# Strassen-like row stage of a float32 block: where the operand sums are made, the order of the products, and who sums the weights

## The chip, the cores and the metric

The kernel runs on one core of a Trainium2 chip. Its time is the device time of the whole program in microseconds (us), the median of several executions.

## The reference, cut to what matters

Three transformer-like blocks run one after the other on x of 1024 positions by 1024 channels, all in float32. The change lies in the first block's feed-forward layer and in the step from there to the second block:

```python
D_FF = 2816
hn = rmsnorm(h, norm_ffn[l])
g, up = jnp.split(hn @ w_ffn_in[l], 2, axis=-1)
h = h + (jax.nn.silu(g) * up) @ w_ffn_out[l]
...
return rmsnorm(h, norm_final)
```

The second block begins with a projection `u = x @ w_in`, whose first column block holds the gates of an mLSTM.

## The kernel before

Activations lie transposed in SBUF: a tile has 128 channels on the partitions and 1024 positions along them. `h` has eight such tiles. Every float32 product is made as three float32r matmuls of 128x128 by 128x512: high part of the weights by high part of the operand, high by low, low by high. ScalarE makes the high part of the weights (`w_hi`, an ACTIVATE copy), GpSimd the low part (`w_lo`, a subtraction), and VectorE the low part of the operand.

**Column pairs (L1587).** The hidden layer is 22 tiles. Two are made in the plain way, the rest in 20 column pairs (a gate and an up block) by seven products on quarter matrices, as Strassen and Winograd do it. `mixed_pair` takes 84 matmuls a pair, twelve a product. Product j waits for `half_split`, GpSimd's low half of its weights; products 2 and 4 also wait until ScalarE has copied a bank away (`snapped`). Four half tiles of weights form a ring. `mixed_pair_scalar` is the order written out for ScalarE: w_hi of products 2 and 3, wait until the hidden tile of the pair before is made (`hid_made`), snapshot 1, then `behind_snap`, then w_hi 4 and 5, snapshot 3, w_hi 6, snapshot 5, w_hi 0 of the next pair, the silu, w_hi 1. The store of the hidden tile to `hid_dram` stands in `behind_snap`. GpSimd's `split_pair` makes three weight sums and seven low halves for each pair. VectorE (`pair_vector`) joins banks and makes the hidden tile, `act_g` for even tiles and `act_h` for odd ones.

**Row stage (L1650).** The second product of the layer, hidden by `w_ffn_out`, is again seven products on quarters: even and odd hidden tiles, low and high positions, even and odd output tiles. Each product i has 11 parts, 77 steps in all, and a step is twelve matmuls (four feature pairs m of three). Weights come in pieces (512 KB for two) through a ring of four blocks. Products 1 to 4 need sums of operand quarters; VectorE makes them in the stage (`sum_part`, L2181 to L2190), from hidden quarters loaded as wholes. Products 1, 2, 4 and 6 need sums of weights, also by VectorE (`sum_weights`, L2204 to L2213). Part and weight tiles are in rings of four: step s is rounded when step s - 3 has begun. When a product is full, `add_product` adds its four banks to h.

**Norm and gates.** ScalarE makes x_hi and the square of each tile of h, VectorE x_lo and the sum of squares; odd tiles come first. TensorE waits until all additions are made (`rows_added`), releases the weights (L531), and makes the gates block and the next block as a pair of interleaved blocks (`feature_pair`, L545), with the mean of the squares (`raw_mean`, L1551) behind tile 6. GpSimd splits both blocks behind the row stage. Behind the mean, ScalarE makes `first_root`, and VectorE scales three tiles of h, then makes `gate_rows` (L2605), on which the next block's bank and the gates' chain (soft, `log_f`, scans) wait.

## Time and profile before

| | |
|---|---|
| median of 3 executions | 3338.17 us (3336.87 to 3340.07) |
| profiled execution | 3340.51 us, span 3338.4 us |
| TensorE busy | 3194.8 us, 96% |
| VectorE, ScalarE, GpSimd busy | 1973.4, 1152.1, 1632.6 us |

The span runs from the first to the last instruction of the profile; times in its views count from its start. PE is TensorE, DVE VectorE, ACT ScalarE, POOL GpSimd, SP the engine that issues most loads; ACTq is the issue of a DMA on ScalarE. An engine's busy share over the whole span says little of a stage, so the rows below are of stages. The column pairs lie at 770 to 1154 us, the row stage at 1157 to 1373, the gates behind it.

### The profile page before, as it was taken

What the parts mean: (1) busy time and instruction counts of PE and PEld (TensorE: products, weight loads), DVE (VectorE), ACT (ScalarE), POOL (GpSimd) and SP (SyncE); (2) the same over time, 40 slices, a digit from 0 to 9 for tenths busy, and PEclk for the clock granted to TensorE, in tenths of its full rate; (3) what the DMA queues carried; (4) which work ended last, traced back from release to release, by engine and by line L of the source; (5) the groups of instructions that cost most, each with busy time, mean ns of one, the idle gap of its engine ahead of it and who ended that gap; (6) DMA issues with size and microseconds to landing.
All of it is one profiled execution on the core that took longest, in us unless ns stands there. A gap on an engine that the chain in (4) does not pass through costs nothing.

```text
span 3338.4 us, 41113 instructions
## 1 busy us (share of the span) xinstructions
PE 3194.8 (96%) x15258; PEld 2532.7 (76%) x15258; DVE 1973.4 (59%) x2372; ACT 1152.1 (35%) x1893; POOL 1632.6 (49%) x975
## 2 busy tenths in 40 slices
PE   8999999989999999889999899999999989999997
PEld 6776678768888778778876678888888858767775
DVE  6325645785333488797866673333333468988735
ACT  5435511043333334433323352222222341333351
POOL 5771134438888755413322147676676743333332
PEclk9999999999999999999999999999999999999998
DMA  3232014112222463131111121111111211111111
GB/s 120 104 116 69 34 49 182 49 33 76 85 84 82 154 212 101 46 95 58 64 37 35 37 82 60 41 60 52 50 58 43 89 51 39 43 43 50 42 32 70
DMA packets 72042, 236.11 MB, mean 71 GB/s; under 512 B 7792, under 2 KB 8432, under 8 KB 70896
## 3 DMA queue, kind: packets, MB, share of 16 engines
q1 hardware_dynamic: 54800, 162.03, 15.2%
q10 hardware_dynamic: 17120, 72.40, 5.8%
q8 instruction: 83, 1.36, 0.2%
q14 instruction: 39, 0.32, 0.0%
HBM read 203.46 MB, written 30.94 MB: 70 GB/s over the span
## 4 chain that ended last, share of the span: by engine, by line
PE 74%; DVE 13%; issue 4%; ACT 4%; POOL 3%; DMA 2%; ACTq 0%; DVEq 0%; POOLq 0%; SPq 0%
PE acc L1587 26%; PE acc L503 24%; PE acc L1603 7%; PE acc L523 5%; PE acc L1650 3%; PE acc L971 2%; PE acc L945 2%; POOL w_lo L3569 1%; DVE conv_slots L3127 1%; PE acc L595 1%; PE acc L545 1%; PE acc L922 1%; POOL raw L3564 1%; ACT band_probs L1086 1%; DVE h L1137 1%
## 5 line engine op out<-in xcount | busy, mean ns | idle before, releaser
L3554 POOL TENSOR_TENSOR w_hi<-raw,zero 128x1024 fp32r<-128x1024 f32 x107 | 219.0, 2047 | 1155.5 <-PE acc L503 551.5
L3569 POOL TENSOR_TENSOR w_lo<-raw,w_hi 128x512 fp32r<-128x512 f32 x318 | 488.5, 1551 | 206.3 <-ACT w_hi L1685 206.0
L1137 DVE TENSOR_TENSOR h<-h,acc 128x1024 f32<-128x1024 f32 x240 | 292.5, 1221 | 163.6 <-PE acc L1603 120.7
L3558 POOL TENSOR_TENSOR w_lo<-raw,w_hi 128x1024 fp32r<-128x1024 f32 x114 | 320.7, 2813 | 105.0 <-ACT w_hi L2522 96.6
L1685 ACT ACTIVATE w_hi<-raw 128x512 fp32r<-128x512 f32 x318 | 191.0, 625 | 410.4 <-POOL raw L3564 148.9
L1587 PE MATMUL acc<-x_hi,w_hi 128*128 128x512 f32 x812 | 316.3, 390 | 4.0 <-POOL w_lo L3569 1.4
L1587 PE MATMUL acc<-x_hi,w_lo 128*128 128x512 f32 x812 | 316.0, 389 | 0.0
L1587 PE MATMUL acc<-x_lo,w_hi 128*128 128x512 f32 x812 | 316.0, 389 | 0.0
L3564 POOL TENSOR_TENSOR raw<-raw 128x512 f32<-128x512 f32 x159 | 241.6, 1520 | 68.8 <-DMA raw<-blocks 58.5
L503 PE MATMUL acc<-x_hi,w_hi 128*128 128x512 f32 x816 | 257.0, 396 | 16.4 <-POOL w_lo L3558 4.5
L1587 PE MATMUL acc<-t_hi,w_hi 128*128 128x512 f32 x672 | 262.3, 390 | 3.4 <-POOL w_lo L3569 2.3
L1587 PE MATMUL acc<-t_lo,w_hi 128*128 128x512 f32 x672 | 261.6, 389 | 0.0
L1587 PE MATMUL acc<-t_hi,w_lo 128*128 128x512 f32 x672 | 261.5, 389 | 0.0
L503 PE MATMUL acc<-x_lo,w_hi 128*128 128x512 f32 x816 | 253.3, 392 | 0.0
L503 PE MATMUL acc<-x_hi,w_lo 128*128 128x512 f32 x816 | 252.8, 391 | 0.0
L3127 DVE SCALAR_TENSOR_TENSOR conv_slots<-conv_slots,par 128x1024 f32<-128x1024 f32 x120 | 227.5, 1896 | 4.1
L503 PEld LDWEIGHTS acc<-x_hi,w_hi 128*128 128x128 f32 x816 | 152.5, 189 | 51.9 <-issue 15.2
L2023 DVE TENSOR_TENSOR act_g<-high_sum,acc 128x512 f32<-128x512 f32 x33 | 22.7, 688 | 274.5 <-ACT high_sum L1693 274.4
L1587 PEld LDWEIGHTS acc<-x_hi,w_hi 128*128 128x128 f32 x812 | 152.4, 188 | 37.2 <-issue 4.1
L503 PEld LDWEIGHTS acc<-x_lo,w_hi 128*128 128x128 f32 x816 | 154.3, 189 | 32.7
L503 PEld LDWEIGHTS acc<-x_hi,w_lo 128*128 128x128 f32 x816 | 154.3, 189 | 32.6
L1587 PEld LDWEIGHTS acc<-x_hi,w_lo 128*128 128x128 f32 x812 | 152.4, 188 | 31.8
(498 smaller groups left out, 6824.7 us busy)
## 6 DMA issues: line engine op xcount, KB each, us to landing
raw<-blocks SPq DMA_DIRECT2D x189, 512.0 KB, 3.6
raw<-blocks SPq DMA_DIRECT2D x106, 256.0 KB, 2.6
raw<-row_pieces SPq DMA_DIRECT2D x22, 512.0 KB, 3.5
piece_block<-row_pieces SPq DMA_DIRECT2D x22, 512.0 KB, 3.5
hid_dram<-act_g ACTq DMA_DIRECT2D x11, 512.0 KB, 2.6
hid_dram<-act_h ACTq DMA_DIRECT2D x10, 512.0 KB, 2.6
h<-x_t ACTq DMA_DIRECT2D x8, 512.0 KB, 8.8
h<-x_t ACTq DMA_DIRECT2D x2, 2048.0 KB, 13.2
```

The costliest lines, as they stand in the source:

```text
L503: ins = pe.matmul(acc[s][:, c], w[:, slot, tile, :], part[:, c], start=(n == 0 and m == 0), stop=(n == last and m == 2))
L523: ins = pe.matmul(acc[s][:, c], w[:, slot, k, :], part[:, k, c], start=(k == 0 and m == 0), stop=(k == KT - 1 and m == 2))
L1137: dve.tensor_tensor(h[:, j, :], h[:, j, :], acc[s], ALU.add).then_inc(acc_free[s], 1)
L1587: ins = pe.matmul(bank, half_tile(w, at_, k), part[:, k, :], start=(begins and k == 0 and m == 0), stop=(k == QUARTER - 1 and m == 2), ski ...
L1603: ins = pe.matmul(acc[s][:, c], half_tile(w, (first + half) % 4, 2 * j + n), part[:, c], start=(n == 0 and m == 0), stop=(n == 1 and m == 2))
L1650: ins = pe.matmul(row_bank(i, m), row_half(w, step, m), x, start=(ROWS_BEGIN[i] and part == 0 and n == 0), stop=(part == ROW_PARTS - 1 and ...
L1685: act.activation(half_tile_range(w_hi, (2 * p + j) % 4), source.rearrange("p (a b) -> p a b", b=P), ACT.Copy)\
L3127: ins = dve.scalar_tensor_tensor(out=out, in0=shifted, scalar=weight, in1=out, op0=ALU.mult, op1=ALU.add)
L3554: pool.tensor_tensor(hi, raw[:, slot, :], nothing, ALU.add).then_inc(hi_split, 1)
L3558: pool.tensor_tensor(lo, raw[:, slot, :], hi.bitcast(F32), ALU.subtract).then_inc(w_split, 1)
L3564: pool.tensor_tensor(out, in0, in1, op).then_inc(sums_made, 1)
L3569: pool.tensor_tensor(half_tile_range(w_lo, at_), halves(source), half_tile_range(w_hi, at_).bitcast(F32), ALU.subtract).then_inc(half_spli ...
```

## The change

The operand sums are made among the column pairs: after every second pair VectorE makes three sums and a difference from the quarters of the two hidden tiles (`sum_hidden`, four operations of 128x512), and ScalarE stores the tiles and the three sums to `hid_dram` (seven slots of 256 KB a part) in three DMAs, behind a wait for `hid_summed`. The last of the eleven is stored by SP. In the row stage each step's operand comes from there through a ring of eight (`load_part`), and no step sums operands.

The order of the steps is a list: products 0 to 4, parts 0 to 2 of product 5, all of product 6, then the rest of product 5, whose weights and operand need no sum. The weight difference of product 6 is made by GpSimd (`sum_pieces`). The last three steps are interleaved by feature pair. Two blocks for the gates are loaded and split during the stage, at steps 36 to 56, into tiles of their own (`first_hi`, `first_lo`). TensorE waits for the additions of six products only and has no release matmul; the mean stands behind tile 4. ScalarE rounds the two blocks that follow before it makes the root, and VectorE scales one tile of h instead of three ahead of `gate_rows`.

```diff
+PART_RING = 8
+ROWS_TOGETHER = 3
+PART_SLOT = (0, 4, 5, 6, 1, 2, 3)
+FIRST_LOADED, FIRST_ROUNDED = (36, 50), (42, 56)
...
+ROW_ORDER = [(i, part) for i, first, after in ((0, 0, ROW_PARTS), (1, 0, ROW_PARTS), (2, 0, ROW_PARTS), (3, 0, ROW_PARTS),
+                                               (4, 0, ROW_PARTS), (5, 0, 3), (6, 0, ROW_PARTS), (5, 3, ROW_PARTS))
+             for part in range(first, after)]
+ROW_DONE = (0, 1, 2, 3, 4, 6, 5)
+
+
+def last_step(i):
+    return ROW_ORDER.index((i, ROW_PARTS - 1))
...
+        hidden_sums = at("hidden_sums", 132, [P, 3, HALF])
+        part_ring = [at(f"early_part{i}", 144 + 2 * i, [P, HALF])[:, :] for i in range(PART_RING)]
+        part_ring += [at(f"part{i}", 24 + 8 * (i // 2) + 2 * (i % 2), [P, HALF])[:, :] for i in range(PART_RING)]
+        late_squares = at("late_squares", 124, [P, KT // 2, TOK])
+        first_stage = at("first_stage", 184, [P, TOK])
+        first_hi = at("first_hi", 160, [P, 2, KT, P], F32R)
+        first_lo = at("first_lo", 168, [P, 2, KT, P], F32R)
...
-            for step in range(ROW_STEPS):
-                i, part = divmod(step, ROW_PARTS)
+            for step in range(ROW_STEPS - ROWS_TOGETHER):
                 if step == ROW_PARTS:
                     pe.wait_ge(snapped, t.count("snap"))
                     pe.wait_ge(joined, t.count("join"))
-                pe.wait_ge(row_split, step + 1)
-                pe.wait_ge(part_made, step + 1)
-                hi, lo = row_part_hi[step % ROW_RING], row_part_lo[step % ROW_RING]
-                for m in range(FEATURE_PAIRS):
+                row_steps(pe, [step])
+            row_steps(pe, range(ROW_STEPS - ROWS_TOGETHER, ROW_STEPS))
+            pe.wait_ge(rows_added, FEATURE_PAIRS * (PRODUCTS - 1))
+
+        def row_steps(pe, steps):
+            for m in range(FEATURE_PAIRS):
+                for step in steps:
+                    i, part = ROW_ORDER[step]
+                    if m == 0:
+                        pe.wait_ge(row_split, step + 1)
+                        pe.wait_ge(part_made, step + 1)
                     if i >= 2 and part == 0:
                         pe.wait_ge(rows_added, FEATURE_PAIRS * (i - 2) + m + 1)
+                    hi, lo = row_part_hi[step % ROW_RING], row_part_lo[step % ROW_RING]
...
+            pe.wait_ge(rows_added, FEATURE_PAIRS * (PRODUCTS - 1))
...
-            def store(n, b):
-                act.dma_start(hid_dram[:, bass.ds(n, 1), :].rearrange("p a n -> p (a n)"), hidden_of[b][:, :])\
-                   .then_inc(hid_out[b], 16)
-
-            def store_first(b):
-                act.wait_ge(hid_made, t.count("hid_made"))
-                store(b, b)
+            def store(part):
+                act.wait_ge(hid_summed, t.next("hid_summed"))
+                for out, (source, first, after) in zip(hid_out, hidden_parts):
+                    act.dma_start(hid_dram[:, bass.ds(part, 1), first:after, :].rearrange("p a b n -> p (a b) n"), source)\
+                       .then_inc(out, 16)
 
             def pair(b, follow, stored, behind_snap=None):
                 def store_last():
-                    if stored is not None:
-                        store(stored, 1 - b)
                     if behind_snap is not None:
                         behind_snap()
+                    if stored is not None:
+                        store(stored)
...
 
-            pair(0, "pair", 1, round_last)
-            pair(1, "pair", 2)
+            pair(0, "pair", 0, round_last)
+            pair(1, "pair", None)
...
-                act.wait_ge(dve_summed, ROW_PARTS * (1, 2, 4, 6).index(i) + part + 1)
+            if i in (1, 2, 4):
+                act.wait_ge(dve_summed, ROW_PARTS * (1, 2, 4).index(i) + part + 1)
+            elif i == 6:
+                act.wait_ge(pool_summed, part + 1)
             else:
                 await_piece(act, row_piece(step))
...
+            act.wait_ge(part_in[step % PART_RING], 16 * (step // PART_RING + 1))
+            act.activation(row_part_hi[step % ROW_RING], part_at(step), ACT.Copy).then_inc(part_high, 1)
+
+        def part_at(step):
+            return part_ring[step if step < PART_RING else PART_RING + step % PART_RING]
+
+        hidden_parts = ((act_g[:, :].rearrange("p (a n) -> p a n", a=2), 0, 2),
+                        (act_h[:, :].rearrange("p (a n) -> p a n", a=2), 2, 4),
+                        (hidden_sums[:, :, :], 4, PRODUCTS))
 
...
+        NORM_STEPS = (62, 64, 66, 68)
 
         def rows_and_norm_scalar(act, t, ch, gain, root, ahead):
             for step in range(ROW_RING, ROW_STEPS):
                 step_high(act, step)
-                if step >= ROW_STEPS - 8 and (ROW_STEPS - step) % 2 == 0:
-                    norm_tile_scalar(act, t, gain, (step - ROW_STEPS + 8) // 2)
+                if step in FIRST_ROUNDED:
+                    first_high(act, FIRST_ROUNDED.index(step))
+                if step in NORM_STEPS:
+                    norm_tile_scalar(act, t, gain, NORM_STEPS.index(step))
...
+        def sum_hidden(dve, t, ch):
+            even_low, even_high = act_g[:, 0:HALF], act_g[:, HALF:TOK]
+            odd_low, odd_high = act_h[:, 0:HALF], act_h[:, HALF:TOK]
+            dve.wait_ge(hid_made, t.count("hid_made"))
+            dve.wait_ge(hid_out[2], t.count("out2") * 16)
+            t.next("out2")
+            ch.link(dve.tensor_tensor(hidden_sums[:, 0, :], odd_high, even_high, ALU.subtract))
+            ch.sync()
+            ch.link(dve.tensor_tensor(hidden_sums[:, 1, :], hidden_sums[:, 0, :], even_low, ALU.add))
+            ch.link(dve.tensor_tensor(even_high, even_high, even_low, ALU.subtract))
+            ch.sync()
+            dve.tensor_tensor(hidden_sums[:, 2, :], odd_low, hidden_sums[:, 1, :], ALU.subtract).then_inc(hid_summed, 1)
...
+            with t.loop(STEPS - 1, snap=6, join=8, prod=2 * PRODUCTS, gated=2, hid_made=2, out0=1, out1=1, out2=1):
                 pair_vector(dve, t, ch, 0)
                 pair_vector(dve, t, ch, 1)
+                sum_hidden(dve, t, ch)
+                ch.reset()
             pair_vector(dve, t, ch, 0)
 
             def first_parts():
-                lower_part(dve, 0)
-                lower_part(dve, 1)
+                for step in range(ROW_RING):
+                    lower_part(dve, step)
 
             pair_vector(dve, t, ch, 1, first_parts)
+            sum_hidden(dve, t, ch)
...
-            for step in range(2, ROW_STEPS):
-                i, part = divmod(step, ROW_PARTS)
+            adds = {}
+            for i in range(PRODUCTS - 2):
+                for m in range(FEATURE_PAIRS):
+                    adds.setdefault(last_step(i) + (4 + m // 2 if i == PRODUCTS - 3 else 4 + m), []).append((i, m))
+            for m in range(FEATURE_PAIRS):
+                adds.setdefault(last_step(PRODUCTS - 1) + 4 + m // 2, []).append((PRODUCTS - 1, m))
+            for step in range(ROW_RING, ROW_STEPS):
                 if step < ROW_STEPS - 1:
                     sum_weights(dve, step + 1)
-                    sum_part(dve, step + 1)
                 lower_part(dve, step)
-                if i and 3 <= part < 3 + FEATURE_PAIRS:
-                    add_product(dve, i - 1, part - 3)
-                if i == PRODUCTS - 1 and part in (4, 6, 8, 10):
-                    lower(part // 2 - 2)
-                if i == PRODUCTS - 1 and part in (7, 9):
-                    sum_square((part - 5) // 2)
-            add_product(dve, PRODUCTS - 1, 0)
+                for i, m in adds.get(step, ()):
+                    add_product(dve, i, m)
+                if step in LOWER_STEPS:
+                    lower(LOWER_STEPS.index(step))
+                if step in SQUARE_STEPS:
+                    sum_square(1 + SQUARE_STEPS.index(step))
+            add_product(dve, PRODUCTS - 2, 0)
             for m in range(FEATURE_PAIRS):
                 if m < FEATURE_PAIRS - 1:
-                    add_product(dve, PRODUCTS - 1, m + 1)
+                    add_product(dve, PRODUCTS - 2, m + 1)
                 else:
-                    sum_square(3)
+                    sum_square(KT // 2 - 1)
                 lower(KT // 2 + m)
...
-            release_next(pe)
             for _ in range(KT):
                 t.next("squared")
-            feature_pair(pe, t, expect_parts(t, KT), lambda: raw_mean(pe, t), KT - 2, True, ODD_FIRST)
+            feature_pair(pe, t, expect_parts(t, KT), lambda: raw_mean(pe, t), KT - 4, False, ODD_FIRST, (first_hi, first_lo))
...
+        def rounded_behind_rows(act, ch):
+            kept_gain(act, ch)
+            round_block(act, BEHIND_1 + 2, BEHIND_1 + 1)
+            round_block(act, BEHIND_1 + 3, BEHIND_1 + 1)
...
-            scale_kept(dve, ch, 0, 3)
+            scale_kept(dve, ch, 0, 1)
             s = await_acc(dve, t)
             dve.tensor_tensor(gate_rows[:, :], acc[s], first_root[:, :], ALU.mult).then_inc(acc_free[s], 1)
-            scale_kept(dve, ch, 3, 4)
+            scale_kept(dve, ch, 1, 4)
...
+            def load_part(step):
+                i, part = ROW_ORDER[step]
+                sp.dma_start(part_at(step), hid_dram[:, part, PART_SLOT[i], :]).then_inc(part_in[step % PART_RING], 16)
 
             def load_row_stage(done):
                 sp.wait_ge(half_split, done + 5)
                 load_pieces(0)
                 sp.wait_ge(prod_full, done + 2)
-                load_parts(even_low_runs, 0, 0, 4, 0, 0, 0, even_low_in[0])
-                load_parts(even_low_runs, 0, 4, 8, 0, 0, 4, even_low_in[1])
+                sp.wait_ge(hid_out[0], 16 * (ROW_PARTS - 1))
+                for step in range(PART_RING // 2):
+                    load_part(step)
                 sp.wait_ge(half_split, done + 6)
                 load_pieces(1)
-                sp.wait_ge(prod_full, done + 3)
-                sp.wait_ge(hid_out[0], 16 * ROW_PARTS)
-                load_parts(even_low_runs, 1, 0, 3, 0, 0, 8, even_low_in[2])
+                for step in range(PART_RING // 2, PART_RING):
+                    load_part(step)
                 sp.wait_ge(prod_full, done + PRODUCTS)
-                load_pieces(2)
-                load_pieces(3)
-                load_parts(even_high_runs, 0, 0, 4, 0, 1, 0, even_high_in[0])
-                sp.wait_ge(hid_made, FFN_TILES)
-                sp.dma_start(hid_dram[:, FFN_TILES - 1, :], act_h[:, :]).then_inc(hid_out[1], 16)
-                load_parts(even_high_runs, 0, 4, ROW_PARTS, 0, 1, 4, even_high_in[1])
-                load_pieces(4)
-                sp.wait_ge(hid_out[1], 16 * ROW_PARTS)
-                at_ = 0
-                for run, tiles in enumerate(odd_high_runs):
-                    count = tiles.shape[1]
-                    load_parts(odd_high_runs, run, 0, count, 1, 1, at_, odd_high_in[at_ >= 6])
-                    at_ += count
-                for block in range(5, ROW_BLOCKS):
+                for block in range(2, ROW_RING):
                     load_pieces(block)
-                    if block in (16, 17, 18):
-                        run = block - 16
-                        load_parts(odd_low_runs, run, 0, odd_low_runs[run].shape[1], 1, 0, (0, 7, 9)[run], odd_low_in)
+                sp.wait_ge(hid_summed, ROW_PARTS)
+                for out, (source, first, after) in zip(hid_out, hidden_parts):
+                    sp.dma_start(hid_dram[:, ROW_PARTS - 1, first:after, :], source).then_inc(out, 16)
+                for out in hid_out:
+                    sp.wait_ge(out, 16 * ROW_PARTS)
+                loaded = ROW_RING
+                for step in range(ROW_STEPS):
+                    while loaded < ROW_BLOCKS and behind_row_block(loaded - ROW_RING) == step + 1:
+                        sp.wait_ge(row_split, step + 1)
+                        load_pieces(loaded)
+                        loaded += 1
+                    for slot in range(2):
+                        if behind_row_block(ROW_BLOCKS - ROW_RING + slot) == step + 1:
+                            sp.wait_ge(row_split, step + 1)
+                            load(slot, BEHIND_1 + 2 + slot)
+                    if step + PART_RING < ROW_STEPS:
+                        sp.wait_ge(part_made, step + 1)
+                        load_part(step + PART_RING)
+                    if step in FIRST_LOADED:
+                        b = FIRST_LOADED.index(step)
+                        sp.wait_ge(w_split, BEHIND_1 + b - PLAIN_2)
+                        sp.dma_start(first_stage[:, :], blocks[BEHIND_1 + b]).then_inc(raw_in[b], 16)
...
+            def sum_pieces(step):
+                i, part = ROW_ORDER[step]
+                if i == 6:
+                    piece = piece_at(row_piece(step))
+                    await_piece(pool, row_piece(step))
+                    pool.wait_ge(dve_summed, ROW_PARTS + part + 1)
+                    pool.tensor_tensor(piece, piece, weight_sums[:, part, :], ALU.subtract).then_inc(pool_summed, 1)
+
             def split_row_stage():
                 for step in range(ROW_STEPS):
+                    if step < ROW_STEPS - 1:
+                        sum_pieces(step + 1)
                     pool.wait_ge(row_high, step + 1)
                     pool.tensor_tensor(half_tile_range(w_lo, (step + 3) % 4), halves(weight_source(step)),
                                        half_tile_range(w_hi, (step + 3) % 4).bitcast(F32), ALU.subtract).then_inc(row_split, 1)
+                    if step in FIRST_ROUNDED:
+                        b = FIRST_ROUNDED.index(step)
+                        pool.wait_ge(hi_split, BEHIND_1 + b + 1 - PLAIN_2)
+                        hi, lo = (w[:, b, :, :].rearrange("p a b -> p (a b)") for w in (first_hi, first_lo))
+                        pool.tensor_tensor(lo, first_stage[:, :], hi.bitcast(F32), ALU.subtract).then_inc(w_split, 1)
```

## Rows read from the trace of the kernel before

**Rows 1.** Windows: busy us (instructions) of each engine, granted TensorE clock, DMA share, GB/s.

```profile
770.00:1154.00 384.00, 383.17 (x1690) 316.96 (x1689) 141.33 (x142) 137.65 (x223) 323.99 (x218) 1.00 0.26 87
...
1183.00:1251.00 68.00, 67.60 (x281) 50.60 (x280) 66.99 (x77) 27.78 (x48) 38.14 (x25) 1.00 0.52 177
```

**Rows 2.** Timeline, TensorE, first matmuls of the row stage: start us, length us, engine, line.

```profile
1156.97 0.47 PE L1650 MATMUL acc<-row_part_hi,w_hi 128*128 128x512 f32 x1 [2.33 <-DVE row_part_lo L2170]
...
1160.92 0.39 PE L1650 MATMUL acc<-row_part_lo,w_hi 128*128 128x512 f32 x1
```

**Rows 3.** Timeline, TensorE, in the last column pair, then in products 1 and 2.

```profile
1127.28 0.39 PE L1587 MATMUL acc<-x_hi,w_hi 128*128 128x512 f32 x1
...
1138.16 0.39 PE L1587 MATMUL acc<-t_hi,w_hi 128*128 128x512 f32 x1
...
1191.80 0.47 PE L1650 MATMUL acc<-row_part_hi,w_hi 128*128 128x512 f32 x1
...
1209.22 0.47 PE L1650 MATMUL acc<-row_part_hi,w_hi 128*128 128x512 f32 x1
```

**Rows 4.** Timeline, TensorE, from the last row matmul on; in brackets idle before, releaser.

```profile
1372.67 0.39 PE L1650 MATMUL acc<-row_part_hi,w_lo 128*128 128x512 f32 x1
...
1377.89 0.79 PE L531 MATMUL acc<-ident,mean_w 128*128 128x128 f32 x2 [4.83 <-DVE h L2224]
...
1384.31 0.72 PE L545 MATMUL acc<-x_hi,w_hi 128*128 128x512 f32 x2 [0.99 <-POOL w_lo L3558]
...
1409.32 0.70 PE L503 MATMUL acc<-x_hi,w_hi 128*128 128x512 f32 x2 [3.92 <-DVE gate_rows L2605]
...
1448.06 1.19 PE L503 MATMUL acc<-x_hi,w_hi 128*128 128x512 f32 x2 [2.57 <-DVE o_gate L2531]
```

**Rows 5.** Timeline, GpSimd, one step of product 1.

```profile
1188.35 1.55 POOL L3626 TENSOR_TENSOR w_lo<-weight_sums,w_hi 128x512 fp32r<-128x512 f32 x1 [1.35 <-ACT w_hi L1875]
```

**Rows 6.** Timeline, VectorE, the same step.

```profile
1188.68 1.77 DVE L2204 TENSOR_TENSOR weight_sums<-piece_block,raw 128x512 f32<-128x512 f32 x1
...
1190.97 0.68 DVE L2170 TENSOR_TENSOR row_part_lo<-even_high,row_part_hi 128x512 fp32r<-128x512 f32 x1
```

**Rows 7.** Timeline, ScalarE, the root behind the norm.

```profile
1399.98 1.12 ACT L711 ACTIVATE first_root<-acc,par 128x1024 f32<-128x1024 f32 x1 [17.77 <-PE acc L1551]
```

**Rows 8.** Timeline, VectorE, gate rows and what follows.

```profile
1407.96 1.21 DVE L2605 TENSOR_TENSOR gate_rows<-acc,first_root 128x1024 f32<-128x1024 f32 x1
...
1414.71 1.22 DVE L2612 SCALAR_TENSOR_TENSOR log_f<-f_rows,soft 64x1024 f32<-64x1024 f32 x1 [2.02 <-ACT soft L2564]
```

**Rows 9.** Timeline, VectorE, the last operation of a column pair.

```profile
1117.71 1.61 DVE L2114 TENSOR_TENSOR act_h<-act_h,snaps 128x1024 f32<-128x1024 f32 x1
```

**Rows 10.** Timeline, GpSimd, around the store in a column pair.

```profile
1121.81 1.29 POOL L3564 TENSOR_TENSOR raw<-raw 128x512 f32<-128x512 f32 x1
...
1124.31 2.53 POOL L3569 TENSOR_TENSOR w_lo<-raw,w_hi 128x512 fp32r<-128x512 f32 x2
```

**Rows 11.** Timeline, ScalarE, around the store, then two DMA issues in a row.

```profile
1119.38 0.60 ACT L1693 ACTIVATE snaps<-acc 128x512 f32<-128x512 f32 x1 [1.40 <-DVE act_h L2114]
...
1123.19 1.16 ACT L1685 ACTIVATE w_hi<-raw 128x512 fp32r<-128x512 f32 x2 [3.21 <-POOL raw L3564]
...
1439.62 0.81 ACTq L2577 DMA_DIRECT2D ends_all<-ends_dram  x2
```

**Rows 12.** Timeline, VectorE, in the first column pair.

```profile
778.50 2.29 DVE L2152 TENSOR_TENSOR x_lo<-two_stages,x_hi 128x2048 fp32r<-128x2048 f32 x1 [2.47 <-ACT x_hi L1854]
```

**Rows 13.** Timeline, ScalarE, in the first column pair.

```profile
780.88 0.60 ACT L1693 ACTIVATE snaps<-acc 128x512 f32<-128x512 f32 x1 [1.08 <-PE acc L1587]
```

**Rows 14.** Timeline, TensorE, a shorter idle time.

```profile
1868.10 0.74 PE L503 MATMUL acc<-att_hi,w_hi 128*128 128x512 f32 x2 [1.96 <-DVE h L1137]
```

**Rows 15.** Windows of 1 us behind two idle times of TensorE.

```profile
1157.60:1158.60 1.00, 1.00 (x4) 0.76 (x3) 1.00 (x2) 0.57 (x2) 1.00 (x2) 0.50 1.02 324
...
1868.00:1869.00 1.00, 0.90 (x4) 0.75 (x5) 1.00 (x2) 0.00 (x0) 0.00 (x0) 1.00 0.00 0
```

145 lines of the change are left out of this document (42 added, 103 removed).

## The prediction

> **What bounds the kernel now.** I read the page first: TensorE is busy for 96% of the span, so only its idle and slow stretches can pay. Windows by stage come next [rows 1]. In the column pairs (770 to 1154 us) TensorE is busy 383.17 of 384 us; the reader is to see that GpSimd is busy 323.99 of the same 384 us (84%) and VectorE only 141.33 (37%). In products 1 and 2 of the row stage (1183 to 1251) VectorE is busy 66.99 of 68 us. The timeline of TensorE shows three places where the stage loses time.
>
> At its start TensorE idles 2.33 us, and then needs 3.95 us for ten matmuls that take 2.27 us in steady state, 1.7 us lost [rows 2]. Steady state is 48 matmuls, or four steps, in 1138.16 - 1127.28 = 10.88 us: 0.227 us a matmul, 2.72 us a step. In products 1 and 2 six steps take 1209.22 - 1191.80 = 17.42 us, 2.90 us each [rows 3]: VectorE makes a weight sum, an operand sum and a low part in each and waits for GpSimd. At the end, the last row matmul starts at 1372.67 and ends at E = 1372.90. Behind it stand idle times of 4.83, 0.99, 3.92 and, at 1448, 2.57 us [rows 4].
>
> How VectorE and GpSimd meet sets the prices. GpSimd's w_lo begins at 1188.35 and ends at 1189.90 [rows 5]; VectorE's operation on two tensors in SBUF, asked for at 1188.68, ends at 1190.45, 0.55 us after it, where one alone takes 0.68 [rows 6]. So the two take turns: about 0.56 us for VectorE, 1.15 for GpSimd, 1.71 for one of each. The Trainium skill, "SBUF — State Buffer", section "🔬 SBUF: two separate sides", calls it an exclusive lock on a shared pair of ports, held for the whole instruction. The trace agrees by the 1.77 us above, and the rule speaks against adding two-tensor operations wherever GpSimd is never idle; the sum by it would be the one made below from the rows.
>
> **The row stage, part by part.** Out of it go 44 operand sums on VectorE, in products 1 to 4. Products 1 and 2 then have two VectorE operations a step and one on GpSimd: 1.15 + 2 x 0.56 = 2.3 us, under 2.72. That gives back about 22 x (2.90 - 2.72) = 4.0 us. In product 6 the subtraction moves to GpSimd: two of its operations and one of VectorE's, 2 x 1.25 + 0.56 = 3.06 us a step against 2.72. Eleven steps fall behind by 3.7 us. The ring of four half tiles lets GpSimd finish about 6 us ahead of need (three steps less its own work), and the first-block split in front of it (step 56) eats some 2.5 of that. So the cost is 0 to 3 us; I take 1, nearer nothing because product 5's rest follows with light steps. The 77 operand loads of 256 KB go through a ring of eight, five or more steps ahead of need: nothing, hidden under matmuls. The reload of pieces and operands now waits behind the stores of the last sums on SP, 1.8 MB: some 6 us behind the sums at about 1165, so about 1173. Step 8 begins at 1156.97 + 1.7 + 8 x 2.72 = 1180.4 and needs load, rounding and low half, about 6 us: 0 to 2 us; I take 0. The stage's start has the same wait as now: nothing. VectorE takes four low parts instead of two ahead of the last pair's product, then the four sums: some 1.7 us for a low part beside GpSimd, so the product is made about 1162.5 and the sums about 1165. Step 4 isn't due before 1156.97 + 1.7 + 4 x 2.72 = 1169.5: nothing. Sum: 3 us gained, between 0 and 4.
>
> **The tail.** The last three steps are interleaved by feature pair, so VectorE's last additions lie 2 us apart under matmuls, and two gate blocks are split ahead. TensorE need not wait: the 4.83 us, the 0.99 and the slow clock behind them go. The mean of squares now stands behind tile 4, 48 matmuls from E: E + 10.9. Its sum needs VectorE's last low part and four additions, about E + 9; two GpSimd splits of the next blocks (about 2.4 us each, twice the half-tile's 1.25) run among them, which makes about E + 13.5. The root is ready some 4 us after the mean starts (matmuls, then two ScalarE operations of about 1.1 us [rows 7]): E + 17.6. The first block is full after 30 more matmuls (6.8 us) and the mean's 1.3: E + 21.6; the gate rows end at E + 22.8. Now they end at 1409.17, and log_f starts 5.5 us later at 1414.71 = E + 41.8 [rows 8]. Changed it starts at about E + 28.3, 13.5 us earlier. That chain also sets the wait at 1448, so it passes on. Without the splits in the way it would be 15.4; with a slow clock behind the wait at the mean, 11.8. I take 13.
>
> **The column pairs.** Added are four half-width sums on VectorE every second pair, three stores instead of two, and a wait: ScalarE now waits for hid_summed right behind its first snapshot, before it rounds the weights of product 4. Queued behind are w_hi of products 4 and 5 and the snapshot that frees the bank; GpSimd waits for the w_hi, and TensorE for GpSimd's low half. Now the hidden tile is made at 1119.32 [rows 9]. From there GpSimd works without a break: low half, sum at 1121.81, a second sum, the low half of product 4 at 1124.31, the first of two in 2.53 us, so done about 1125.6 [rows 10]. ScalarE's w_hi comes at 1123.19 [rows 11]; TensorE needs that half at 1127.28 [rows 3]. Slack: 1.7 us. With the four sums taking turns with GpSimd: the low half under way when they are asked for ends at 1120.5 (the next one, 1.25 long, now ends right before 1121.81), and four times 0.56 with three turns of 1.15 between is 5.7: 1126.2. Then three DMA issues at 0.4 us (two take 0.81 [rows 11]) to 1127.5; w_hi to 1128.1; low half to 1129.4. TensorE gets it at about 1129.5: 2.2 us late. Nine of the ten stores in ScalarE's queue are such. In the first pair VectorE is at its x_lo until 780.79 [rows 12], and the second snapshot at 780.88 [rows 13] puts TensorE's product 4 at about 783.6. GpSimd's turn ends at 781.9 and the sums at 784.4; with issues, w_hi and low half 787.4: 3.8 us late. Bounds for the nine: 0 (sums without contention: 2.5 us, done at 1121.9, ahead of w_hi's own time), and 2.5.
>
> **The clock.** Behind the idle 2.33 us the granted clock was 0.50, the 1.2 GHz level, and cost 1.7 us; behind 1.96 us [rows 14] it was 1.00 [rows 15]. Nine idle times of about 2.1 by the profile's measure lie between, nearer the latter: I take no drop there, and 1.7 us at the first. Loss in the pairs: 9 x 2.2 + 3.8 + 1.7 = 25.3; with a drop each time 15.3 more.
>
> **Sum.** -3 - 13 + 25.3 = +9.3 us. The profiled execution took 3340.5 us (span 3338.4), so 3349.8; its like on the median of 3338.2 is 3347.5.
>
> **Rivals.** (1) *The sums don't delay ScalarE.* If hid_summed comes within 4.2 us of the hidden tile (1127.28 less low half, w_hi and three issues is 1123.5), no late half: -16 and at most a few us for the first pair, 3322 to 3327; I name 3323. For it: VectorE is idle 63% of the stage. Against: GpSimd has no gap in just those microseconds. This is the case of the other sign. (2) *Half the delay*: VectorE gets two sums in one turn, each store costs 1.1 us; 9.9 + 5.5 - 16 = -0.6: 3337.6. (3) *The clock falls at each wait*: +24.6, 3363. (4) *GpSimd bounds product 6*: if the lead is gone before it, 3.7 us are lost instead of 1: +12, 3350. The Trainium skill, "GPSIMD Engine Reference", section "3.1 Elementwise — side-by-side cycle accounting", gives a GpSimd add at 1.96 times VectorE's time, which speaks against the move; the rows agree with 1.29 [rows 10] to 0.68 [rows 6].
>
> **Chances.** Forecast 0.36, (1) 0.31, (2) 0.13, (3) 0.14, (4) 0.06. A difference under 0.2% (6.7 us) can't be told from none: (2) whole, and a third of the forecast's band, where the delay or the tail comes out better, make 0.23; slower 0.44; faster, (1) and the good end of (2), 0.33. The range runs from under (1) to (3): 3320 to 3364, with under 2 in 10 outside. The forecast's own range is 3340 to 3355.
>
> **What would show it.** In the pairs: TensorE idle about 2 us in front of product 4 in every second pair, released by GpSimd's w_lo, with ScalarE waiting for hidden_sums; VectorE's sums at 1.7 us each. If they take 0.7 and TensorE's stage stays at 383 of 384, the loss falls and (1) holds. Row stage: steps of 2.72 in products 1 and 2; no idle time at product 6. Tail: the gates' first matmul right behind the last row matmul, log_f about 28 us behind E. Most likely to make me wrong is the order in which VectorE and GpSimd get their turns.

## The result, and the profile after

The changed kernel takes **3379.0 us** (median of 4, 3377.8 to 3383.0) beside 3337.6 us for the kernel before on the same chip: ratio 1.0125, 95% interval 1.0107 to 1.0142. It is slower by 41 us. 3347.5 was forecast, with a range to 3364. The profiled execution took 3379.3 us, its span 3377.6, 39.2 more than before.

The windows of TensorE show where. First the column pairs, in the same 384 us as [rows 1]; then three stretches of 4 us, each right behind one of its idle times; then the row stage.

```profile
770.00:1154.00 384.00, 351.73 (x1469) 285.25 (x1468) 182.77 (x158) 117.89 (x193) 294.08 (x192) 0.95 0.26 90
1005.05:1009.05 4.00, 4.00 (x17) 3.30 (x18) 0.29 (x1) 1.05 (x3) 2.44 (x2) 1.00 0.98 358
1048.69:1052.69 4.00, 4.00 (x10) 3.13 (x11) 0.00 (x0) 0.10 (x1) 2.38 (x2) 0.50 0.96 363
1092.69:1096.69 4.00, 4.00 (x9) 3.14 (x10) 0.00 (x0) 0.13 (x1) 2.42 (x2) 0.50 1.00 368
...
1211.15:1426.35 215.20, 211.96 (x924) 174.41 (x925) 158.85 (x150) 98.84 (x163) 129.64 (x88) 0.99 0.61 204
```

TensorE issued 1469 matmuls in the 384 us where it issued 1690. Two things are to be seen. It is idle for 32 us, and in 4 busy microseconds behind two of the three waits it gets through 9 or 10 matmuls instead of 17: busy, at a granted clock of 0.50 (the column behind the five engines). The first row matmul starts at 1211.15 instead of 1156.97, 54.2 us later. Summed over the timeline, 34.5 us of that are additional idle time and 17.0 us slow matmuls behind eight of the waits. Another 1.6 us are the ends of the ten matmuls in front of the long waits: idle time is counted from the end of a matmul, 0.39 us behind its start, where in the steady state the next starts after 0.23. 1.1 us is not assigned.

The idle times have one form. This is the timeline of TensorE at four of its ten waits before product 4, and at one of the shorter ones that follow them:

```profile
787.48 0.77 PE L1601 MATMUL acc<-x_hi,w_hi 128*128 128x512 f32 x1 [4.89 <-POOL w_lo L3581]
...
1005.05 0.50 PE L1601 MATMUL acc<-x_hi,w_hi 128*128 128x512 f32 x1 [2.94 <-POOL w_lo L3581]
...
1018.19 0.50 PE L1601 MATMUL acc<-t_hi,w_hi 128*128 128x512 f32 x1 [1.42 <-POOL w_lo L3581]
...
1092.69 0.79 PE L1601 MATMUL acc<-x_hi,w_hi 128*128 128x512 f32 x1 [2.91 <-POOL w_lo L3581]
...
1179.70 0.50 PE L1601 MATMUL acc<-x_hi,w_hi 128*128 128x512 f32 x1 [3.04 <-POOL w_lo L3581]
```

The ten waits before product 4 come to 31.3 us: 4.89 in the first pair, then 2.91 to 3.04. Five shorter ones add 4.0. Behind eight of the ten the clock fell, for 6 to 14 matmuls at 0.43 us.

One store shows the chain. ScalarE, then VectorE, then GpSimd, in the timeline between 1080 and 1094:

```profile
1081.78 0.60 ACT L1713 ACTIVATE snaps<-acc 128x512 f32<-128x512 f32 x1 [1.38 <-DVE act_h L2127]
1088.64 0.34 ACTq L1836 DMA_DIRECT2D hid_dram<-act_g  x1
1089.14 0.34 ACTq L1836 DMA_DIRECT2D hid_dram<-act_h  x1
1089.63 0.85 ACTq L1836 DMA_DIRECT2D hid_dram<-hidden_sums  x1
1090.67 1.15 ACT L1705 ACTIVATE w_hi<-raw 128x512 fp32r<-128x512 f32 x2 [8.29 <-issue]
```
```profile
1080.06 1.61 DVE L2127 TENSOR_TENSOR act_h<-act_h,snaps 128x1024 f32<-128x1024 f32 x1
1081.70 1.66 DVE L2137 TENSOR_TENSOR hidden_sums<-act_h,act_g 128x512 f32<-128x512 f32 x1
...
1086.80 1.67 DVE L2142 TENSOR_TENSOR hidden_sums<-act_h,hidden_sums 128x512 f32<-128x512 f32 x1
```
```profile
1086.17 1.74 POOL L3576 TENSOR_TENSOR last_sum<-raw 128x512 f32<-128x512 f32 x1
1091.38 2.50 POOL L3581 TENSOR_TENSOR w_lo<-raw,w_hi 128x512 fp32r<-128x512 f32 x2 [3.46 <-ACT w_hi L1705]
```

The hidden tile ends at 1081.67 and the fourth sum at 1088.47. ScalarE stands from 1082.4 to 1088.6; then it issues three DMAs, the last for 0.85 us, and w_hi starts at 1090.67, 2.2 us behind the sums. GpSimd, which had no gap there before [rows 10], now idles 3.46 us for w_hi, and TensorE starts product 4 at 1092.69. The profile puts the 8.29 us down to "issue": the wait stands in front of a DMA issue, which isn't counted as work.

In the row stage products 1 and 2 run at 2.72 us a step. But three waits are new: 1.78 us in front of step 8, 0.66 in front of step 71 and 0.79 at the start of the three last steps. The stage is 215.0 us long from its first matmul to the start of its last, 215.7 before.

```profile
1236.55 0.47 PE L1671 MATMUL acc<-row_part_hi,w_hi 128*128 128x512 f32 x1 [1.78 <-DVE row_part_lo L2200]
...
1426.12 0.39 PE L1671 MATMUL acc<-row_part_hi,w_lo 128*128 128x512 f32 x1
...
1440.16 3.68 PE L1565 MATMUL acc<-rstd,mean_w 128*128 128x512 f32 x4 [2.76 <-DVE rstd L2251]
```

E is now 1426.35. Of [rows 4] the 4.83 and 0.99 are gone; the mean waits 2.76 us, and its four matmuls and those behind it run slowly (3.68 us for four). On VectorE, against [rows 8]:

```profile
1450.72 1.23 DVE L2619 TENSOR_TENSOR gate_rows<-acc,first_root 128x1024 f32<-128x1024 f32 x1 [3.32 <-PE acc L559]
1457.78 1.21 DVE L2626 SCALAR_TENSOR_TENSOR log_f<-f_rows,soft 64x1024 f32<-64x1024 f32 x1
1459.02 2.28 DVE L2631 TENSOR_TENSOR_SCAN m_rows<-log_f,gate_rows 32x1024 f32<-32x1024 f32 x1
```

log_f starts at E + 31.4 (E + 41.8 before). So the account at log_f is 54.2 - 0.7 - 10.4 = 43.1 us, and 3.9 of it are given back later. 2.1 of these come in the next operation: the scan m_rows took 4.37 us before, as VectorE's line of the kernel before shows, and takes 2.28 after. GpSimd's line shows what was different: before, the low half of a block ran from 1415.63 to 1418.19, and the scan ended 2.14 us behind it, about its own length when nothing runs beside it. In the changed kernel GpSimd's splits end at 1436.36, ahead of the scan. So the scan seems to have waited for a turn too; no run tested this.

```profile
1415.96 4.37 DVE L2617 TENSOR_TENSOR_SCAN m_rows<-log_f,gate_rows 32x1024 f32<-32x1024 f32 x1
```
```profile
1415.63 2.56 POOL L3558 TENSOR_TENSOR w_lo<-raw,w_hi 128x1024 fp32r<-128x1024 f32 x1 [9.87 <-ACT w_hi L2522]
```

### The profile page after: what moved, and what is told of

Its sections match the earlier page's. It is cut to its first block, busy times and chain, and to the rows that moved or that the text cites. A ratio compares the mean times of both kernels' runs of the same rounds, so it can differ in the third digit from the quotient of the medians.

```text
span 3377.6 us, 41203 instructions
## 1 busy us (share of the span) xinstructions
PE 3207.3 (95%) x15256; PEld 2541.3 (75%) x15256; DVE 1999.9 (59%) x2361; ACT 1150.9 (34%) x1895; POOL 1649.0 (49%) x984
## 4 chain that ended last, share of the span: by engine, by line
PE 67%; POOL 11%; DVE 10%; issue 7%; ACT 3%; DMA 1%; ACTq 0%; POOLq 0%; DVEq 0%; SPq 0%
PE acc L515 24%; PE acc L1601 16%; PE acc L1617 7%; POOL w_lo L3581 5%; PE acc L535 5%; PE acc L1671 4%; POOL raw L3576 3%; PE acc L985 2%; PE acc L559 2%; PE acc L959 2%; DVE conv_slots L3141 1%; PE acc L609 1%; PE acc L936 1%; POOL last_sum L3576 1%; ACT band_probs L1100 1%
## 5 line engine op out<-in xcount | busy, mean ns | idle before, releaser
L1601 PE MATMUL acc<-x_hi,w_hi 128*128 128x512 f32 x812 | 324.9, 400 | 35.8 <-POOL w_lo L3581 33.2
L515 PE MATMUL acc<-x_hi,w_hi 128*128 128x512 f32 x816 | 255.8, 395 | 10.1 <-POOL w_lo L3570 4.5
L1601 PEld LDWEIGHTS acc<-x_lo,w_hi 128*128 128x128 f32 x812 | 156.8, 193 | 32.6
L1601 PEld LDWEIGHTS acc<-x_hi,w_lo 128*128 128x128 f32 x812 | 156.1, 192 | 33.4
L515 PEld LDWEIGHTS acc<-x_lo,w_hi 128*128 128x128 f32 x816 | 153.6, 188 | 32.4
```

Source lines behind the costliest of these rows:

```text
L515: ins = pe.matmul(acc[s][:, c], w[:, slot, tile, :], part[:, c], start=(n == 0 and m == 0), stop=(n == last and m == 2))
L1601: ins = pe.matmul(bank, half_tile(w, at_, k), part[:, k, :], start=(begins and k == 0 and m == 0), stop=(k == QUARTER - 1 and m == 2), ski ...
```

## The experiments

Four suspects stood in one place of the column pairs: the four sums beside GpSimd, ScalarE's wait for them, ScalarE's three issues, and the bytes that leave. The experiments take them apart. The kernel before took 3338.8 to 3339.1 us on the chips of these runs.

**e3_sums_alone.** The sums with nothing behind them, in the kernel before:

```
+            ch.link(dve.tensor_tensor(hidden_sums[:, 0, :], odd_high, even_high, ALU.subtract))
...
+            ch.link(dve.tensor_tensor(hidden_sums[:, 3, :], even_high, even_low, ALU.subtract))
...
+                sum_hidden(dve, t, ch)
```

> The kernel before with the four half-width VectorE operations added behind every second column pair (ten times), written into unused memory; nothing waits for them and nothing stores them. Theory A: only GpSimd's turns are lost, 2.2 us against a slack of 1.7: 0 to 6 us slower than before, 3338 to 3344 us, with VectorE's sums at about 1.7 us each. Theory B (the sums themselves are the cause): 25 to 50 us slower, over 3360 us.

3345.5 us (10 runs), ratio 1.0019 (1.0010 to 1.0029): 6.4 us slower than before, 1.5 above the end of theory A's range and far from theory B's. In the profile the row stage starts at 1159.91, 2.9 us later than before, with idle times of 0.2 to 0.9 us in the pairs, and the span is 4.1 us longer. The sums take turns with GpSimd, as forecast, but this alone is a small part of the loss.

**e1_store_late.** Wait and stores move from behind snapshot 1 to behind product 6's high half:

```
             weights_high(act, t, p, 6, free)
+            if behind_last is not None:
+                behind_last()
             take_snap(act, t, 5, high_sum[:, :])
...
-                mixed_pair_scalar(act, t, 0, FREE_BEHIND_PAIR, follow, gate, behind_snap=store_last,
+                mixed_pair_scalar(act, t, 0, FREE_BEHIND_PAIR, follow, gate, behind_snap=behind_snap, behind_last=store_last,
```

> The changed kernel with one edit: in the column pairs ScalarE waits for the sums and issues their three stores behind the w_hi of product 6 instead of behind its first snapshot. Theory A (what stands behind the wait on ScalarE makes GpSimd's low half of product 4 late, and the clock falls behind the idle time): the nine idle times of 2.9 us go; GpSimd is still pushed back four turns of 0.56 us, 2.2 us against a slack of 1.7, so at most 0.5 to 1 us is left of each. Column pairs some 45 to 50 us shorter than in the changed kernel, total 3327 to 3335 us. Theory B (the four sums on VectorE themselves hold GpSimd up, wherever the store stands): the idle times stay near 2 us, total over 3360 us.

3359.1 us (3354.6 to 3363.8), ratio 1.006 (1.0043 to 1.0076). That is 20 us better than the changed kernel and 20 worse than before: a miss. The waits before product 4 are 0.3 us or gone, as expected, but new ones, most of 1.5 to 3.6 us, stand in front of product 0 of the next pair. Its timeline on GpSimd and on SP's queue shows a cause that none of the theories had:

```profile
1076.10 1.30 POOL L3576 TENSOR_TENSOR raw<-raw 128x512 f32<-128x512 f32 x1 [4.20 <-DMA raw<-blocks]
```
```profile
1067.91 0.33 SPq L3432 DMA_DIRECT2D raw<-blocks  x1
1069.59 0.33 SPq L3428 DMA_DIRECT2D raw<-blocks  x1
1070.83 0.33 SPq L3436 DMA_DIRECT2D raw<-blocks  x1
```

In this kernel ScalarE issues its stores at 1068.43, 1068.93 and 1069.43, in the very microseconds in which SyncE asks for the next pair's 1 MB of weights. GpSimd waits 4.20 us for its block (3.7 to 5.7 in the nine pairs of this kind, 4.4 on average). Before, the same wait was 1.40 us (1.3 to 1.9, 1.6 on average), as the kernel before's line shows:

```profile
1072.38 1.29 POOL L3564 TENSOR_TENSOR raw<-raw 128x512 f32<-128x512 f32 x1 [1.40 <-DMA raw<-blocks]
```

**e2_wait_kept.** The wait stays behind snapshot 1 and only the issues move to behind product 6's high half:

```
+                def wait_summed():
...
+                    if stored is not None:
+                        act.wait_ge(hid_summed, t.next("hid_summed"))
+
+                def store_last():
+                    if stored is not None:
+                        store(stored)
...
+                mixed_pair_scalar(act, t, 0, FREE_BEHIND_PAIR, follow, gate, behind_snap=wait_summed, behind_last=store_last,
```

> The changed kernel with ScalarE's wait for the sums left behind its first snapshot, and only the three DMA issues moved behind the w_hi of product 6. It splits the delay of product 4 into the wait and the issues. The traces put 1.4 us of sums behind w_hi's own time and 2.0 us of issues between the last sum and w_hi. Theory A with both parts: idle times of about 1 us in place of 2.9, too short for the clock to fall: total 3335 to 3345 us. If the issues alone are the delay, it equals the run with the whole store late (3327 to 3335). If the issues are free beside the wait, it stays at 3370 to 3380.

3377.1 us, ratio 1.0116: also a miss in its time. But it prices the wait. TensorE idles 0.90 us before product 4 in place of 2.9 (3.13 in place of 4.89 in the first pair); the remainder comes back as 2.1 to 3.5 us in front of product 0 of the next pair, where the issues and their bytes now are.

```profile
1084.60 0.50 PE L1601 MATMUL acc<-x_hi,w_hi 128*128 128x512 f32 x1 [0.90 <-POOL w_lo L3586]
```

**e7_two_issues.** The changed kernel, its wait kept in place, with the third store put off by one pair (store_of issues one of the three):

```
             def store(part):
                 act.wait_ge(hid_summed, t.next("hid_summed"))
-                for out, (source, first, after) in zip(hid_out, hidden_parts):
...
+                store_of(part, 0)
+                store_of(part, 1)
...
                     if stored is not None:
                         store(stored)
+                    if third is not None:
+                        store_of(third, 2)
```

> The changed kernel with its wait and its place kept, but the 768 KB store of the three sums issued one pair later, behind snapshot 1 of the next odd tile: behind the wait stand two issues instead of three. Theory A, ScalarE's own issue time is what makes w_hi late on top of the wait: the third issue took 0.85 us and began 0.5 us after the second, so the weight behind it starts about 1.3 us after the sums instead of 2.2, TensorE's idle before product 4 falls from 2.9 to about 2.0 us, the low clock behind it stays away more often, and the time falls by 9 to 20 us, to 3359 to 3370. Theory B, the wait alone counts and the issues run beside it: no change, 3376 to 3382.

3363.6 us in its one run, inside theory A's 3359 to 3370. The same wait of TensorE is 1.91 us:

```profile
1078.55 0.50 PE L1601 MATMUL acc<-x_hi,w_hi 128*128 128x512 f32 x1 [1.91 <-POOL w_lo L3587]
```

So the idle time before product 4 is 0.90 us with the wait alone, 1.91 with two issues behind it, and 2.91 with three. In the first pair it is longer, 3.13, 4.07 and 4.89 us, and the clock fell behind all three. In the nine other pairs the clock fell behind none of the waits without issues (0.76 to 1.03 us), four with two issues (1.68 to 1.94), and seven with three (2.91 to 3.04).

**e8_late_two.** As e1_store_late, but the third store one pair later, behind snapshot 1 (the same edit as above): 1.0 MB in place of 1.79 beside the weights.

> The stores of act_g and act_h behind product 6's high half (as in e1_store_late, 3359), the 768 KB store of the sums one pair later behind snapshot 1. Theory A, traffic: in e1_store_late 1.79 MB left in the same microseconds in which 1 MB of weights came in, and GpSimd waited 4.2 us for its block (1.4 before); with 1.0 MB there the wait falls to about 3 us, TensorE's idle before product 0 from 1.7 to about 0.5 us, and the time to 3343 to 3350. Theory B, ScalarE's issue time: at that place ScalarE waits 4.2 us for TensorE behind the issues anyhow, but the third issue's 0.85 us is gone from the product's chain: idle falls by under 0.3 us, 3355 to 3360.

3353.7 us in one run: 5 us better than e1_store_late, but outside both ranges. GpSimd's wait for its block hardly shrank. In the nine pairs of this kind it is 3.3 to 4.5 us, 4.0 on average, where e1_store_late had 4.4 and theory A expected 3:

```profile
1073.36 1.29 POOL L3586 TENSOR_TENSOR raw<-raw 128x512 f32<-128x512 f32 x1 [4.32 <-DMA raw<-blocks]
```

The DMA view of 1062 to 1078 of e8_late_two, with each queue's share, suggests why: between 1066.8 and 1072 the sixteen engines are at 90% or more in all slices but one, shared by both queues. Weights of 1 MB are held up while stores go out beside them, and 1.0 MB of stores lasts about as long as the weights do, so more stores add little. This reading is argued; no run varied the size of the load.

```profile
DMA  0000000000479999999979999511000000000000
...
q1 hardware_dynamic: 432, 1.05, 20.9%
q10 hardware_dynamic: 288, 1.05, 17.1%
```

**e12_before_late.** The timing of the bytes by itself: the kernel before, with no sums and no new wait, and its 512 KB store of each hidden tile moved to behind product 6's high half.

```
                 def store_last():
                     if stored is not None:
                         store(stored, 1 - b)
-                    if behind_snap is not None:
-                        behind_snap()
...
+                mixed_pair_scalar(act, t, 0, FREE_BEHIND_PAIR, follow, gate, behind_snap=behind_snap, behind_last=store_last,
```

> The kernel before with one edit: its 512 KB store of each hidden tile is issued behind product 6's high half instead of behind snapshot 1. No sums, no new wait; only the moment changes, so that the store leaves beside the 1 MB of weights that SyncE asks for there. Theory A, the two queues share the DMA engines evenly while both have work: e1_store_late (1.79 MB) and e8_late_two (1.0 MB) both had GpSimd wait 4.2 to 4.3 us for its block, 2.8 to 2.9 more than before, because 1 MB of loads is held up by at most 1 MB of stores; 0.5 MB at about 400 GB/s holds them up by about 1.3 us, the wait goes from 1.4 to about 2.7 us in every pair, and since about 1.1 us of that is slack before product 0, TensorE idles 0.1 to 0.4 us a pair: 3340 to 3347. Theory B, the load was late in those kernels for another reason (SyncE released late): the wait stays at 1.4 us and the time at 3336 to 3341.

3355.7 us in one run, against 3338.8 before: the mechanism is theory A's, and it costs more than A said. GpSimd's wait is 2.3 to 3.3 us in all pairs but the first, 3.0 on average (A said about 2.7), and TensorE idles 0.83 to 1.28 us at fourteen places (at one before); the row stage starts 15.3 us later. SyncE didn't ask later: from its first load to GpSimd's start it takes 6.7 us in the second pair shown, 5.0 in the kernel before, and the 512 KB load lands 5.4 us after it is issued in place of 3.7.

```profile
1046.16 1.29 POOL L3564 TENSOR_TENSOR raw<-raw 128x512 f32<-128x512 f32 x1 [3.21 <-DMA raw<-blocks]
1066.27 1.30 POOL L3564 TENSOR_TENSOR raw<-raw 128x512 f32<-128x512 f32 x1 [3.15 <-DMA raw<-blocks]
```

The same bytes, stored some 6 us later in the pair, cost 17 us.

**e9_spread.** The three stores apart, at moments when SyncE asks for nothing:

```
                     if stored is not None:
+                        store_of(stored, 1)
+                        act.wait_ge(even_summed, t.next("even_summed"))
+                        store_of(stored, 0)
+                    if third is not None:
+                        act.wait_ge(hid_summed, t.next("hid_summed"))
+                        store_of(third, 2)
...
+            dve.tensor_tensor(even_high, even_high, even_low, ALU.subtract).then_inc(even_summed, 1)
             ch.link(dve.tensor_tensor(hidden_sums[:, 1, :], hidden_sums[:, 0, :], even_low, ALU.add))
-            ch.link(dve.tensor_tensor(even_high, even_high, even_low, ALU.subtract))
```

> The stores spread: act_h behind snapshot 1 with no wait of its own (it was waited for already), act_g right behind it once the difference of its two halves is made, which now stands second among the four sums (about 3.4 us after the hidden tile; ScalarE is idle there for 3.9 us), and the three sums one pair later behind snapshot 1. Nothing is issued when the weights of the next pair are asked for. Theory A (wait plus traffic were the whole loss, the sums themselves cost what e3_sums_alone showed, 2.9 us up to the row stage): row stage starts near 1160, and with its 0.7 and the tail's 10.4 us gained and about 3.9 given back behind it the time is 3331 to 3338. Theory B, the pairs have no room for 0.75 MB more of DMA and 6.7 us more of VectorE per two tiles wherever they stand: 3345 to 3360.

3331.8 us (10 runs), ratio 0.998 (0.997 to 0.999) against before, and 47 us under the changed kernel with the same work in it. Theory A holds. GpSimd's wait for its block is 1.2 to 2.1 us, nearly as before. The window of the pairs is nearly that of [rows 1] again, and the row stage starts at 1158.90:

```profile
770.00:1154.00 384.00, 380.70 (x1668) 311.68 (x1668) 211.15 (x179) 132.83 (x220) 336.81 (x217) 1.00 0.30 105
```

On ScalarE one pair looks like this; both waits end inside time in which it has nothing else to do:

```profile
1044.06 0.34 ACTq L1835 DMA_DIRECT2D hid_dram<-act_h  x1
1047.34 0.34 ACTq L1835 DMA_DIRECT2D hid_dram<-act_g  x1
1048.36 1.15 ACT L1705 ACTIVATE w_hi<-raw 128x512 fp32r<-128x512 f32 x2 [3.86 <-POOL raw L3582]
...
1063.77 0.34 ACTq L1835 DMA_DIRECT2D hid_dram<-hidden_sums  x1
```

w_hi waits for GpSimd's sum, as before [rows 11], and no longer for the issues.

**e4_rounds_behind_root.** In the tail of the changed kernel, ScalarE's rounding of two feature blocks behind the root instead of in front of it:

```
             kept_gain(act, ch)
-            round_block(act, BEHIND_1 + 2, BEHIND_1 + 1)
-            round_block(act, BEHIND_1 + 3, BEHIND_1 + 1)
...
+            round_block(act, BEHIND_1 + 2, BEHIND_1 + 1)
+            round_block(act, BEHIND_1 + 3, BEHIND_1 + 1)
```

> The changed kernel with ScalarE's rounding of the two blocks behind the gates' pair moved behind the root, so that GpSimd's two splits no longer stand among VectorE's sums of squares. Theory: in the tail VectorE's squares took 9.4 us for four because GpSimd had its turns between, and TensorE waited 2.76 us for the mean with the clock down behind it. Expected: no wait at the mean, sum of squares done about 9 us behind the last row matmul, 4 to 6 us faster than the changed kernel: 3373 to 3375 us. Rival (the squares wait for ScalarE, not for GpSimd): no change, 3378 to 3380 us. If the third block's split then comes too late, the gain is given back there.

3372.7 us in one run, 6 us under the changed kernel and 0.3 under the 3373 that was the near end of what was expected. That it came so near is in part luck: 2.5 us of it lie in the pairs, where the code is the same (the row stage starts at 1208.68), and 2.0 in the row stage, at whose start the clock didn't fall here. The edit's own part is read at log_f: it starts at E + 26.7 in place of E + 31.4, 4.7 us sooner. 2.5 us of the gain are given back behind it. The wait of 2.76 us at the mean is gone, and with it the slow matmuls behind it. GpSimd's splits of those blocks wait for ScalarE's rounding, so they come later too, and VectorE's four additions of squares have nobody to take turns with: 5.21 us instead of 9.42. VectorE in the changed kernel, then in this one:

```profile
1430.68 9.42 DVE L2251 TENSOR_TENSOR rstd<-rstd,late_squares 128x1024 f32<-128x1024 f32 x4
```
```profile
1426.25 5.21 DVE L2251 TENSOR_TENSOR rstd<-rstd,late_squares 128x1024 f32<-128x1024 f32 x4
```

**e10_spread_root.** e9_spread with that edit.

> e9_spread (3331.8) with ScalarE's rounding of the two blocks behind the root, without the reloads put ahead: it parts e11_spread_all's 7.3 us under e9_spread into the two edits. Theory A, the parts add as their waits do (2.76 us at the mean with up to 1.3 us of slower matmuls behind it; 1.65 us at step 8): 3325 to 3328, 1 to 2 us above e11_spread_all. Theory B, the reload edit brought nothing: 3323 to 3325.

3329.0 us (10 runs), ratio 0.9971 (0.9962 to 0.9981), just above theory A's 3325 to 3328. log_f starts at E + 26.7, 4.6 us sooner than in e9_spread, and the row stage is 2.0 us shorter: here the clock didn't fall at its start, and waits of 0.80 and 0.20 us stand at steps 4 and 8 in place of 1.65 at step 8. Most of that doesn't show in the total, because this kernel's row stage starts at 1165.03, that of e9_spread at 1158.90 and that of e11_spread_all at 1161.64, with the same code in the pairs: idle times of 0.8 to 1.1 us come in some pairs and not in others.

**e11_spread_all.** The last step: SyncE loads the first reloads of the row stage ahead of its wait for the last sums.

```
+                sp.wait_ge(part_made, 1)
+                load_part(PART_RING)
+                sp.wait_ge(row_split, 2)
+                load_pieces(ROW_RING)
+                sp.wait_ge(part_made, 2)
+                load_part(PART_RING + 1)
                 sp.wait_ge(hid_summed, ROW_PARTS)
```

> e9_spread with ScalarE's rounding of the two feature blocks put behind the root of the norm (as in e4_rounds_behind_root, 6 us), and with the first two reloads and block 4 of the row stage issued by SyncE ahead of its wait for the last stores (the 1.78 us wait at step 8). Theory A, the gains add up: 6 to 8 us under e9_spread, 3324 to 3332. Theory B, the reload wait comes back a step later and only the root's part is left: 4 to 6 us under e9_spread.

3324.5 us (4 runs), ratio 0.9958 (0.9941 to 0.9975): the fastest, 14.6 us under before and 54.5 under the changed kernel. The wait at step 8 is gone. Against e9_spread, whose row stage also began with slow matmuls, the stage is 1.95 us shorter (212.92 in place of 214.87 us), and only the reload edit touches it: that is its worth. It is as long as in e10_spread_root (212.89), which had 1.0 us of waits more and was spared the slow matmuls. The 4.5 us between the two kernels lie mostly in the pairs, where their code is the same, and the intervals of the two overlap; they are not shown to be the edit's.

## Why the prediction was wrong

The sign and the place were right: TensorE idle in front of product 4 in every second pair, released by GpSimd's w_lo, with ScalarE at the sums. The size was not: 25.3 us were forecast for the pairs and 54.2 came, and the tail brought 10.4 where 13 were counted.

**The sums beside GpSimd: right.** Done 6.9 us behind the hidden tile was forecast, 6.8 measured, at 1.66 to 1.78 us each. Rival 1, that they don't delay ScalarE, is out. e3_sums_alone shows the turns cost 2.9 us when nothing waits for them.

**The issues: the first mis-sized term.** "Three DMA issues at 0.4 us" took the forecast from 1126.2 to 1127.5, 1.3 us; from the last sum to w_hi it took 2.2. The pair of issues in [rows 11] gave too small a price: here the second starts 0.5 us behind the first, and the third, 768 KB, takes 0.85. That makes 2.2 us late into about 3 late; e7_two_issues confirms it by taking one away, 1.2 us from the last sum to w_hi and 1.0 less idle time. Ten waits come to 31.3 us where 23.6 were counted, and the five shorter ones behind them (4.0 us) were not in the sum at all.

**The clock: the step that failed.** "I take no drop there" rested on one idle time of 1.96 us that had none behind it [rows 14, 15], on waits counted too short. The clock fell behind eight of ten, and cost 17.0 us in place of 1.7. The bound was in the text (15.3 more) and rival 3 named it, at a chance of 0.14; that the difference is 15.3 too is chance, eight falls at 2.1 us in place of nine at 1.7. The account: 25.3 + 7.7 (longer waits) + 4.0 (shorter ones) + 15.3 (clock) - 0.8 (an idle time that before had in this stage too) = 51.5 of 54.2 us, and 1.6 more are the ends of the matmuls in front of the ten waits.

**The row stage: the gain was right, a bound was met.** Without its waits the stage is 3.6 us shorter (4.0 forecast for products 1 and 2), and product 6 has no idle time (1 us forecast), which ends rival 4. But the reload behind SyncE's stores cost 1.78 us. It was bounded at 0 to 2 and taken as 0. SyncE's first reload went out at 1229.48, 18.3 us behind the stage's start where 16 were forecast (1173 less 1157), and load, rounding and low half took 7.1 us, not 6; the step was due at 23.6. 0.66 and 0.79 near the end weren't foreseen. The 0.66 may be product 6's cost after all: GpSimd is busy from 1361.7 to 1406.0 with one gap of 0.42 us, and VectorE's two x_lo ahead of step 71's low part take 2.31 us each, where one takes 1.27 at 1414.59; no run tested it. 0.7 us of the gain is left.

**The tail: mostly right.** The mean came at E + 13.8 (13.5). The slow clock behind its wait was the lower bound of 11.8, and the rest was 1.4 us worse: 10.4. The splits "in the way" were priced at 15.4 - 13.5 = 1.9 us. e4_rounds_behind_root and e10_spread_root show 4.7 and 4.6 at log_f, because it isn't the delay alone but the clock behind it; without the splits log_f comes 15.1 us sooner than before, near the 15.4 forecast.

**What no step had.** When a transfer leaves, and beside what. The prediction checked that the stores were issued by someone and what queued behind them, but not which loads they would share the DMA engines with. In the changed kernel this is the lesser part, at most the shorter waits of 4.0 us. It decided what each repair was worth: e2_wait_kept, with the wait's price down to 0.9 us, was 2 us faster than the changed kernel, less than the runs of either differ among themselves.

Open is why the clock falls behind one wait and not behind another of the same length, and why kernels with the same code in the pairs differ by up to 6 us there. Each kernel has one profile, and the ten runs of e9_spread alone lie 10.7 us apart, so such a difference need not belong to the kernel.

## What to carry to other kernels

A wait on an engine that also prepares the next product must be placed where that engine would be idle anyway, and every DMA that it issues behind the wait counts, here 0.5 to 1 us each; a store that needs new results can go out in pieces, each when it is ready, or one pair later. Before moving a store, look at when the loads that the critical engine waits for are asked for (the timelines of both queues show it). Where TensorE gets a wait that comes again and again, count the slower matmuls behind it as well as the wait: here they added half as much again.

## What the runs showed of the hardware

- The clock behind an idle time of TensorE isn't given by its length alone. The twelve profiles have 133 waits of TensorE of 0.6 us or more between 770 and 1260. Behind the 71 under 1.8 us the clock never fell, behind the 56 of 1.8 to 3.3 us it fell 37 times, and behind the six of 3.5 to 4.9 us each time. The start of the row stage is the same place in all twelve, behind 2.33 to 2.69 us of idle time: nine had slow matmuls there, e4_rounds_behind_root, e7_two_issues and e10_spread_root (2.35, 2.35, 2.36 us) had none. These three wait 0.78 to 0.80 us at step 4 instead, so part of what a slow start costs is hidden. Two windows of 4 us from the first row matmul, of e9_spread and then of e10_spread_root:

```profile
1158.90:1162.90 4.00, 4.00 (x12) 3.19 (x13) 4.00 (x4) 0.04 (x1) 2.68 (x2) 0.65 0.47 190
```
```profile
1165.03:1169.03 4.00, 4.00 (x18) 3.31 (x19) 4.00 (x4) 0.79 (x3) 2.73 (x3) 1.00 0.45 181
```

- A DMA issue on ScalarE isn't one price. The same 768 KB store took 0.80 to 1.09 us as the third of three in a row behind the wait, 0.34 to 0.79 as the third of three in e2_wait_kept, where ScalarE has weights to round beside it, and 0.34 alone, one pair later (e9_spread). What sets the price stays open. Issues in a row start 0.4 to 0.5 us apart.
- What a load of 1 MB loses beside a store grows less and less with the store: GpSimd waited 1.6 us for its block on average without a store beside it (the kernel before), 3.0 beside 0.5 MB (e12_before_late), 4.0 beside 1.0 MB (e8_late_two) and 4.4 beside 1.79 MB (e1_store_late).
